# First gather of both MoE stages in four pieces, first two expert steps one expert at a time

## The reference

```python
x = layer_norm(ALPHA * x + att, ln1_g[layer], ln1_b[layer])
expert, gate = route(h, w_router, b_router)          # top 2 of 16, group limited
# for each expert, on the tokens routed to it:
y = (silu(xblk @ w_gate[e]) * (xblk @ w_up[e])) @ w_down[e]
x = layer_norm(ALPHA * x + ffn, ln2_g[layer], ln2_b[layer])
```

## Time and profile before

| what | value |
|---|---|
| median of 3 runs | 2743.56 us (2742.93 to 2745.32) |
| profiled execution | 2747.91 us, span 2746.0 us |
| PE busy | 2601.8 us (95%) |
| DMA moved | 685.34 MB, mean 250 GB/s |
| granted clock of TensorE | 0.993 on average |

### The profile page before, as it was taken

The page is one execution under the profiler, slowest core; times in us unless marked ns, Lnnn a source line. Parts: engine busy times, 40 slices in busy tenths (PEclk is TensorE's granted clock), DMA queues, the critical chain, the costliest instruction groups (busy, mean ns, idle before and its releaser), DMA issues.

```text
span 2746.0 us, 46041 instructions
## 1 busy us (share of the span) xinstructions
PE 2601.8 (95%) x19583; PEld 2011.6 (73%) x19583; DVE 1273.3 (46%) x1873; ACT 820.2 (30%) x1044; POOL 0.2 (0%) x4
## 2 busy tenths in 40 slices
PE   9999988889999988899999999999999999999998
PEld 9834433357543433399899889999899998999998
DVE  4611100056410101255658765655555668666555
ACT  4300000035100000233443442533433444423433
POOL 0000000000000000000000000000000000000000
PEclk9999999999999999999999999999999999999999
DMA  8999999975999999955654431455555544323454
GB/s 275 354 387 425 425 426 426 427 278 217 370 423 425 426 426 426 366 165 188 220 169 134 128 124 34 153 185 184 181 188 184 181 138 139 108 79 123 154 184 138
DMA packets 290641, 685.34 MB, mean 250 GB/s; under 512 B 14184, under 2 KB 219808, under 8 KB 241696
## 3 DMA queue, kind: packets, MB, share of 16 engines
q1 hardware_dynamic: 285336, 673.37, 65.4%
q10 hardware_dynamic: 5128, 9.37, 0.9%
HBM read 681.65 MB, written 1.05 MB: 249 GB/s over the span
## 4 chain that ended last, share of the span: by engine, by line
PE 75%; DMA 15%; DVE 5%; ACT 2%; issue 1%; SPq 1%; DVEq 0%; ACTq 0%; POOLq 0%
PE psum L423 74%; DMA arena<-in_w_gate 6%; DMA weight_ring<-in_w_gate 4%; DMA arena<-in_w_up 2%; PE psum L431 1%; DVE weight_ring_parts L2349 1%; DMA arena<-in_w_down 1%; DMA weight_ring<-in_w_down 1%; DMA x_chan<-in_w_gate 1%; ACT weight_ring_parts L2341 1%; DVEq L556 0%; DMA weight_ring<-in_w_in_a 0%; DMA weight_ring<-in_w_in 0%; SPq L2137 0%; DVE arena L3544 0%
## 5 line engine op out<-in xcount | busy, mean ns | idle before, releaser
L423 PE MATMUL psum<-weight_ring_parts,arena_parts 128*128 128x256 f32 (+1 forms) x2992 | 666.0, 314 | 1.4 <-ACT arena L791 0.9
L2349 DVE TENSOR_TENSOR weight_ring_parts<-weight_ring,weight_ring_parts 128x2048 fp32r<-128x2048 f32 x217 | 496.5, 2290 | 337.8 <-ACT weight_ring_parts L2341 331.6
L423 PE MATMUL psum<-x_chan_parts,weight_ring_parts 128*128 128x256 f32 x3200 | 610.5, 281 | 9.8 <-DVE arena_parts L2438 5.1
L423 PE MATMUL psum<-arena 64*64 64x64 f32 (+6 forms) x4852 | 560.4, 349 | 41.1 <-DMA arena<-in_w_up 11.6
L2341 ACT ACTIVATE weight_ring_parts<-weight_ring 128x2048 fp32r<-128x2048 f32 x217 | 415.1, 1914 | 467.3 <-POOLq L536 349.3
L423 PEld LDWEIGHTS psum<-weight_ring_parts,arena_parts 128*128 128x128 f32 x2992 | 496.0, 189 | 37.9 <-issue 2.3
L423 PEld LDWEIGHTS psum<-x_chan_parts,weight_ring_parts 128*128 128x128 f32 x3200 | 507.6, 189 | 15.2 <-issue 9.9
L423 PEld LDWEIGHTS psum<-arena 64*64 64x64 f32 (+3 forms) x4852 | 276.7, 141 | 280.3 <-issue 256.8
L423 PE MATMUL psum<-weight_ring,arena 128*64 128x512 f32 (+1 forms) x1664 | 410.0, 578 | 36.9 <-DMA weight_ring<-in_w_gate 12.6
L423 PE MATMUL psum<-weight_ring_parts,x_chan_parts 128*128 128x256 f32 x2336 | 427.4, 285 | 1.8 <-DVE arena_parts L2438 1.7
L423 PE MATMUL psum<-arena_parts,weight_ring_parts 128*128 128x256 f32 x1536 | 418.0, 282 | 0.3 <-DVE arena_parts L2442 0.3
(11 more groups left out here) (330 smaller groups left out, 1836.1 us busy)
## 6 DMA issues: line engine op xcount, KB each, us to landing
weight_ring<-in_w_in SPq DMA_DIRECT2D x70, 1024.0 KB, 5.2
arena<-in_w_up SPq DMA_DIRECT2D x64, 1024.0 KB, 25.7
weight_ring<-in_w_gate SPq DMA_DIRECT2D x64, 1024.0 KB, 25.6
weight_ring<-in_w_up SPq DMA_DIRECT2D x64, 1024.0 KB, 25.6
weight_ring<-in_w_down SPq DMA_DIRECT2D x64, 1024.0 KB, 25.6
arena<-in_w_gate SPq DMA_DIRECT2D x50, 1024.0 KB, 23.9
arena<-in_w_down SPq DMA_DIRECT2D x45, 1024.0 KB, 25.8
weight_ring<-in_ffa_w_in SPq DMA_DIRECT2D x44, 1024.0 KB, 7.5
```

Of the source, the lines that this page charges most:

```text
L423: return nc.tensor.matmul(*args, **kw)
L2349: nc.vector.tensor_tensor(ring_parts[:, sl, :], ring[:, sl, :], f32(HIGH[buf]), ALU.subtract).then_inc(s_split, 1)
```

## The change

- PE (`begin_first`, `gather_two`): the first gather of a stage goes into four banks, 4 products each. Three are done at the start, the fourth between the first and the second expert's products of gate's step 0.
- PE (`step_by_expert`): gate's and up's step 0 of the first pair do the four products of expert 0, then those of expert 1; each expert's last product counts in `s_half`.
- ACT and DVE: copy two banks of two chunks each in place of one bank of four.
- POOL: the first four counts give back one slot each (`steps_done(4, 1)`), then four steps give two each.
- SP: spare 3 is issued after four transfers that need a slot (w_down j = 1 of both, then in layer 0 w_down j = 2 and one of gate, in layer 1 two of gate); before it came after two.

```diff
--- before.py
+++ after.py
@@ -1704,6 +1704,21 @@
                     pe.e.wait_ge(s_free[b], pe.emptied())
                 return opened
 
+            def step_by_expert(j, opened, act, between=None):
+
+                for e in range(2):
+                    slot = pe.job()
+                    pe.e.wait_ge(s_slot[slot], pe.landed())
+                    rows = column_halves(EXPERT_ROWS[slot])
+                    for kk in range(2):
+                        for half in range(2):
+                            last = pe.mm(ps[e * CAP:(e + 1) * CAP, opened[half], :],
+                                         act[:, 2 * j + kk, e * CAP:(e + 1) * CAP], rows[half][:, kk, :],
+                                         start=(j == 0 and kk == 0), stop=False)
+                    last.then_inc(s_half, 1)
+                    if e == 0 and between is not None:
+                        between()
+
             def step(j, opened, act, spares=(None, None)):
 
                 rows = []
@@ -1751,6 +1766,28 @@
                 last.then_inc(s_full[b], 1)
                 return pe.pieces.n - 1
 
+            def gather_two(i, b=None):
+
+                if b is None:
+                    b = pe.take()
+                    pe.e.wait_ge(s_free[b], pe.emptied())
+                for kk in range(2):
+                    for t in range(T):
+                        last = pe.mm(ps[:, b, kk * P:(kk + 1) * P], pair_rows(X[:, t, :], i * 2 + kk), PM[:, t, :],
+                                     start=(t == 0), stop=(t == T - 1))
+                last.then_inc(s_full[b], 1)
+
+            def begin_first():
+
+                for i in range(3):
+                    gather_two(i)
+                fourth = pe.take()
+                pe.e.wait_ge(s_free[fourth], pe.emptied())
+                fourth_piece = pe.pieces.n - 1
+                gate = two_pieces()
+                step_by_expert(0, gate, XG, lambda: gather_two(3, fourth))
+                return gate, fourth_piece
+
             def read(piece):
                 pe.e.wait_ge(s_free[piece % BANKS], pe.read_out(piece))
 
@@ -1765,7 +1802,10 @@
 
                 gate, second_half = begun
                 up = two_pieces()
-                step(0, up, XG)
+                if first:
+                    step_by_expert(0, up, XG)
+                else:
+                    step(0, up, XG)
                 for j in range(1, 4):
                     if j == 2:
                         read(second_half)
@@ -1826,7 +1866,7 @@
 
             pe_keep_busy(1)
             pe.e.wait_ge(s_v2p, pe.c["v2p"].next())
-            rest(begin([gather(0), gather(1)]), True)
+            rest(begin_first(), True)
             rest(down(first=True))
 
             def body(i):
@@ -1870,15 +1910,17 @@
                 else:
                     s.skip()
 
-            b = s.take()
             s.e.wait_ge(s_load["route_bias_cols"], 16 + 16 * 2 * LAYERS)
-            s.e.wait_ge(s_full[b], s.filled())
-            for k in range(4):
-                gain, bias = (GATHER_COLS[:, 2 * l + x, k:k + 1] for x in range(2))
-                last = nc.scalar.activation(XG[:, k, :], ps[:, b, k * P:(k + 1) * P], ACT.Identity,
-                                            scale=gain, bias=bias)
-            last.then_inc(s_free[b], 1)
-            s.skip()
+            for i in range(2):
+                b = s.take()
+                s.e.wait_ge(s_full[b], s.filled())
+                for kk in range(2):
+                    k = 2 * i + kk
+                    gain, bias = (GATHER_COLS[:, 2 * l + x, k:k + 1] for x in range(2))
+                    last = nc.scalar.activation(XG[:, k, :], ps[:, b, kk * P:(kk + 1) * P], ACT.Identity,
+                                                scale=gain, bias=bias)
+                last.then_inc(s_free[b], 1)
+            s.skip(2)
             pair(False)
 
             s.e.wait_ge(s_full[(s.pieces.n - 1) % BANKS], s.filled())
@@ -2058,15 +2100,20 @@
             nc.vector.tensor_reduce(CNT[:, 4:5], CNT[:, 1:SEQ // CAP], AX.X, ALU.add)
             v.sync()
             nc.vector.tensor_copy(NPASS[0:1, 0:1], CNT[0:1, 4:5]).then_inc(s_nb, 1)
-            v.skip()
+            v.skip(2)
             b = v.take()
             v.e.wait_ge(s_load["route_bias_cols"], 16 + 16 * 2 * LAYERS)
             v.e.wait_ge(s_full[b], v.filled())
-            for k in range(4):
-                gain, bias = (GATHER_COLS[:, 2 * l + x, 4 + k:5 + k] for x in range(2))
-                last = nc.vector.tensor_scalar(XG[:, 4 + k, :], ps[:, b, k * P:(k + 1) * P], gain, bias,
-                                               ALU.mult, ALU.add)
-            last.then_inc(s_free[b], 1)
+            for i in range(2):
+                if i == 1:
+                    b = v.take()
+                    v.e.wait_ge(s_full[b], v.filled())
+                for kk in range(2):
+                    k = 4 + 2 * i + kk
+                    gain, bias = (GATHER_COLS[:, 2 * l + x, k:k + 1] for x in range(2))
+                    last = nc.vector.tensor_scalar(XG[:, k, :], ps[:, b, kk * P:(kk + 1) * P], gain, bias,
+                                                   ALU.mult, ALU.add)
+                last.then_inc(s_free[b], 1)
             v_gain_and_bias(4 + 4 * l)
             v.sync()
             nc.vector.nop().then_inc(s_gained, 1)
@@ -2081,7 +2128,7 @@
 
         def g_moe(l):
             g.stage(f"moe{l}")
-            g.skip(8 + 2)
+            g.skip(8 + 4)
 
             def steps_done(n, ring_jobs=2):
                 for _ in range(n):
@@ -2100,7 +2147,8 @@
                 g.freed(2, 2)
                 g.freed(2, 2)
 
-            steps_done(6)
+            steps_done(4, 1)
+            steps_done(4)
             g.skip(2)
             g.freed(2, 2)
             g.skip(6)
@@ -2136,11 +2184,9 @@
                 sp.wait_slot()
                 sp.e.dma_start(EXPERT_ROWS[sl], src).then_inc(s_slot[sl], 16)
 
-            def gate_and_up(pr):
-                for j in range(4):
-                    for w in ("w_gate", "w_up"):
-                        for e in range(2):
-                            one(w, e, j, pr)
+            def gate_and_up(pr, first=0, last=16):
+                for j, w, e in [(j, w, e) for j in range(4) for w in ("w_gate", "w_up") for e in range(2)][first:last]:
+                    one(w, e, j, pr)
 
             def down(pr, first=0, last=4):
                 for j in range(first, last):
@@ -2213,10 +2259,10 @@
                 for e, i in enumerate(down_spares(l, j)):
                     if i is None:
                         one("w_down", e, j, 0)
-                if j == 1:
-                    sp.e.wait_ge(s_gained, l + 1)
-                    spare(3, "w_down", 1, 3)
-            gate_and_up(1)
+            gate_and_up(1, last=l + 1)
+            sp.e.wait_ge(s_gained, l + 1)
+            spare(3, "w_down", 1, 3)
+            gate_and_up(1, first=l + 1)
             steps = later_pairs(sp)
             with sp.e.Fori(0, steps) as i:
                 sp.enter(f"moe{l}", (i, 1))
```

## The result

The changed kernel takes 2752.54 us (median of 13 runs), the one before 2745.32 (13 runs beside them): ratio 1.0024, 95% interval 1.0015 to 1.0032, 7.2 us slower (the interval is 4 to 9 us). The forecast was slower by 8.1. A second set of 11 runs gave 1.0026 (1.0016 to 1.0036), 7.7 us. The profiled execution has a span of 2752.5 us.

What follows compares the result with a forecast made beforehand. The prediction took the DMA stream of expert weights to bound both MoE stages. Losses of 2.8 us in layer 0 and 5.3 in layer 1 gave + 8.1 on a median of 2743.56, so 2751.6 us, range 2748 to 2755.5.

Steps and rivals of the forecast that it cites:

- Bound by the stream: Both MoE stages: each ends when its weight bytes have been moved, so its length is bytes over rate plus idle time.
- Gather in pieces: Start of each MoE stage: copies hide behind later gather pieces, so gate's first expert starts 0.75 us earlier.
- One expert alone runs at 0.43 a record: First steps of gate and up: eight lone records take as long as sixteen paired ones, 3.42 us.
- Gather between the experts, changes of shape: Gate's step 0: fourth gather piece costs 1.01 us plus 0.14 and 0.21 for two changes of shape.
- Border between experts, 0.10 between starts: Between experts on opposite array halves: next expert's first record starts 0.10 us after the last record's start; bounds 0.01 and 0.43.
- R3 and R4: Slot releases seen by SP after up's first and second expert in layer 0, forecast at 148.73 and 151.82 us.
- Restart, + 2.8: Weight stream after the first gather, each layer: single releases leave it short of work, losing 2.8 us; bounds 2.0 and 3.8.
- Second stall: Layer 1, up step of pair 1: TensorE 6.44 us late against slack 1.1 empties the stream, raising the loss to 5.3.
- Restart only: Rival, chance 0.15: layer 1's second stall doesn't come because the queue covers it; + 5.6 us, 2749.2.
- The first release decides: Rival, chance 0.09: lone records at 0.21 us bring the first release 2.4 us earlier; - 4.8 us, 2738.8.
- TensorE slower still: Rival, chance 0.05: lone expert's weight loads aren't hidden and borders don't overlap, TensorE 11.9 late; + 19 us, 2762.6.
- Nothing: Rival, chance 0.06: queue's backlog refills what is held up, or stage ends hang on TensorE; - 0.8 to 0, about 2743.

Runs made afterwards that it cites:

- paired_again: Second run of paired (changed kernel's four-piece gather, both first steps with experts in pairs, slots given back two at a time): 2745.45 us, ratio to before 0.9994.
- the second profile: Profile of the changed kernel run again without any edit, beside the kernel with paired steps: 2753.43 us, ratio to before 1.0026.
- by_expert: Changed kernel's one-expert-at-a-time first steps with single slot releases, but the gather in two pieces as before the change: 2749.64 us, ratio to before 1.0016.
- paired_late: The paired kernel with seven extra products of zeros on TensorE ahead of j = 2 of the first pair: 2752.16 us, executed once.
- paired: Changed kernel with experts in pairs again in both first steps, slots given back two at a time, up's first width half first: 2746.40 us, ratio to before 1.0003.
- changed: The kernel with the whole change described, against the kernel before: 2752.54 us, ratio 1.0024.
- pair_release: Changed kernel with the slots of both experts given back together after the second expert: 2755.62 us, executed once.
- swapped: As pair_release, but up does expert 1 ahead of expert 0: 2756.53 us, executed once.

## Why the prediction was right

The time lay 0.9 us from the forecast, and the two places of the loss were the forecast ones. The mechanism was right; that the size came so close is in part luck, as the last two terms show. Step by step:

- *Bound by the stream.* Right: what is lost in the first 80 us is never made up, and the two stages are longer by 8.8 us in the first profile and 7.1 in the second, where the sets of runs have 7.2 and 7.7.
- *Gather in pieces, + 0.75.* Right: 3.25 against 3.96; paired_again shows it alone, as 0.6 us of stream in layer 0.
- *One expert alone runs at 0.43 a record.* Right: eight in 3.4 us.
- *Gather between the experts, changes of shape.* 0.14 + 1.01 + 0.21 = 1.36 forecast; measured from 136.83 + 3.42 = 140.25 to 141.51, 1.26: right.
- *Border between experts, 0.10 between starts.* This term was mis-sized. The other half's first record starts 1.77 us behind the start of this half's eight, with the fifth of them, while some 1.7 us of this half are still to run. The memory attention's heads have only four records each, and there the next head's first record came behind the fourth; that row didn't carry to eight, and why isn't shown. So R3 and R4 came 1.4 and 2.7 us earlier than forecast and TensorE was 4.1 late, not 6.44.
- *Restart, + 2.8.* Measured 2.2 and 2.1, 2.5 in the second profile. With the real releases the reckoning of the prediction gives 1.5: the second megabyte can flow at 11.66 + 1.70 = 13.36 after the gather, against 9.40 + 2.46 = 11.86 before. The other 0.6 to 1.0, and by_expert's 0.8, is a stream that comes back slowly: from 148 to 154 us it moves 365, 373 and 410 GB/s, worth 0.6 us, with two to five transfers under way. The prediction had no term for it. Why it does so isn't shown: before, with two transfers issued together, it ran at 426 GB/s from 144 us on the earlier trace rows, and two or more were under way there too.
- *Second stall, + 2.5, to 5.3 in layer 1.* Measured 3.1, to 5.3, and in the second profile 2.0, to 4.6. The size is right by two errors that cancel, which is luck. Lateness was 2.3 less, and the slack of 1.1 read off a landing of 6.0 us is really about none: over nine profiles, layer 1's loss follows TensorE's lateness: 0.6 and 0.8, 2.1 and 2.1, 3.4 and 3.4, 3.9 and 4.1, 4.1 and 4.2, 4.1 and 4.6, 4.1 and 5.3, 5.6 and 5.9, 5.7 and 5.7. The 0.94 at 356 GB/s in the earlier trace rows was a sign of it. Why the same lateness of 4.1 once costs 5.3 and once 4.2 stays open. In layer 0 the slack is about 3.9 - 2.1 = 1.8 (paired_late), not 3.7.
- *Rivals.* "Restart only" falls by the window at 780. "The first release decides" needed lone records at 0.21 and falls by the eight in 3.4 us. "TensorE slower still" falls, since weight loads of a lone expert stay hidden (0.43 a record). "Nothing" falls by the time, 4 to 9 us over before by the interval.

## What to carry to other kernels

Splitting a step so that its buffers come back one by one is worth something only if the engine does the first part in less time than both together; where two halves of the array work side by side it doesn't, and the later releases pay. Where a stream is the bound, count its bytes at fixed distances from a landmark in both traces: that finds fractions of a microsecond, and every hole in it. An engine far from the bound may be late only by the thinnest lead anywhere behind; look for windows in which the stream's rate sags more than its share.

## What the runs showed of the hardware

- Products on different halves of the array overlap at a border, although they are issued one after the other: of two sets of eight records of 512 columns the second starts with the fifth of the first, 1.77 us behind its start and not 3.42. By the difference of two kernels the lead is 1.66 us.
- In the first microseconds behind a hole, with two to four megabyte transfers under way, the stream showed a share of 0.95 to 1.01 at 324 to 373 GB/s, where a full one shows 1.01 at 425. The share alone hides this loss. It doesn't come behind every hole: before, it was 426 at once.
- TensorE's granted clock was at half for 3.4 us at the first gather in some executions of a kernel and not in others of the same kernel (paired, paired_again). In layer 0 what the engine had done before was alike: busy 1.08 and 1.85 us of the 2 us windows from 130 and 132 us in paired, in paired_again and in the changed kernel (1.09 and 1.85 before). In layer 1 all four kernels that had it showed another stretch of half clock some 13.6 us earlier (paired: 0.52 and 0.63 in the windows from 701 and 703 us), changed and paired_again had neither, and pair_release and swapped had only the earlier one. Each time it made the gather 1.5 us longer, as much as the whole gain that was to be had.
